# Attention's value product as two split float32r products on paired value halves, with row sums added up on GpSimd

## The reference, cut to what matters

```python
s_s = jnp.einsum('nqhd,nqkd->nqhk', q, ksel).astype(jnp.float32) * scale
p_s = masked_softmax(s_s, smask)
o_s = jnp.einsum('nqhk,nqkd->nqhd', p_s.astype(vsel.dtype), vsel)
...
o_w = jnp.einsum('nqhk,nkd->nqhd', p_w.astype(vw.dtype), vw)
return gates[..., 0:1] * o_c + gates[..., 1:2] * o_s + gates[..., 2:3] * o_w
```

## Time and profile before

| what | value |
|---|---|
| median of 3 runs | 2151.63 us (2148.56 to 2152.69) |
| profiled execution | 2151.09 us |
| its span | 2149.5 us |
| PE busy in the span | 1888.5 us (88%) |
| DVE, ACT, POOL busy | 1066.5, 616.8, 153.6 us |
| attention stage in the span | 1283 to 1745 us |

### The profile page before, as it was taken

How to read it: one execution, slowest core, us unless ns; L and a number is a source line. 1 busy time by engine, 2 the same in 40 slices (tenths; PEclk the granted TensorE clock), 3 DMA queues, 4 the chain that set the end, 5 groups by cost and what they waited for, 6 DMA issues and landing times. The chain is left out here.

```text
span 2149.5 us, 24334 instructions
## 1 busy us (share of the span) xinstructions
PE 1888.5 (88%) x8663; PEld 1347.1 (63%) x8663; DVE 1066.5 (50%) x2180; ACT 616.8 (29%) x1112; POOL 153.6 (7%) x264
## 2 busy tenths in 40 slices
PE   6799999999999999619996947899999978876999
PEld 1588878877877787406555633444445447875886
DVE  1376648746864775504464675455555422213332
ACT  3324343435334331303302522233333310002110
POOL 2101110000000000012210000000000021000000
PEclk9799999999999999857997667899999975557999
DMA  7537555545454544255223000000000032005331
GB/s 239 184 113 237 196 182 186 200 149 194 163 178 137 186 167 157 75 107 175 58 70 99 25 19 18 11 11 10 11 11 0 1 98 83 23 2 199 128 132 62
DMA packets 138776, 230.61 MB, mean 107 GB/s; under 512 B 14439, under 2 KB 90889, under 8 KB 138184
## 3 DMA queue, kind: packets, MB, share of 16 engines
q1 hardware_dynamic: 109525, 158.36, 23.1%
q0 software_dynamic: 17552, 57.22, 7.3%
q10 hardware_dynamic: 11579, 13.48, 2.0%
HBM read 175.27 MB, written 56.15 MB: 108 GB/s over the span
## 5 line engine op out<-in xcount | busy, mean ns | idle before, releaser
L578 PE MATMUL ps<-h_hi,w_hi 128*128 128x512 f32 x832 | 340.7, 410 | 0.0
L580 PE MATMUL ps<-h_lo,w_hi 128*128 128x512 f32 x832 | 325.1, 391 | 0.0
L579 PE MATMUL ps<-h_hi,w_lo 128*128 128x512 f32 x832 | 324.6, 390 | 0.0
L2114 PE MATMUL ps<-pT,values 128*65 128x512 f32 x412 | 216.8, 609 | 0.0
L2176 ACT ACTIVATE pT<-ps 128x512 f32<-128x512 f32 x206 | 123.0, 597 | 294.2 <-PE ps L2101 194.4
L2256 DVE TENSOR_REDUCE part_max<-ps 128x1 f32<-128x512 f32 (+3 forms) x272 | 143.0, 557 | 124.0 <-PE ps L2129 49.6
L920 DVE SCALAR_TENSOR_TENSOR c_acc<-c_u,par,c_acc 128x512 f32<-128x512 f32 x240 | 180.0, 750 | 6.8
L578 PEld LDWEIGHTS ps<-h_hi,w_hi 128*128 128x128 f32 x832 | 157.2, 189 | 35.9 <-issue 6.3
L579 PEld LDWEIGHTS ps<-h_hi,w_lo 128*128 128x128 f32 x832 | 157.1, 189 | 35.4 <-issue 5.8
L580 PEld LDWEIGHTS ps<-h_lo,w_hi 128*128 128x128 f32 x832 | 156.5, 188 | 34.0
L1344 PE MATMUL ps<-rawT,w 128*128 128x254 f32 (+1 forms) x320 | 137.5, 590 | 0.0
(11 more groups left out here) (594 smaller groups left out, 3170.6 us busy)
## 6 DMA issues: line engine op xcount, KB each, us to landing
w_hi<-split_weights SPq DMA_DIRECT2D x78, 512.0 KB, 3.7
w_lo<-split_weights SPq DMA_DIRECT2D x78, 512.0 KB, 4.6
w_raw<-in_w_in SPq DMA_DIRECT2D x26, 512.0 KB, 4.6
split_weights<-w_hi POOLq DMA_DIRECT2D x26, 512.0 KB, 5.5
split_weights<-w_lo POOLq DMA_DIRECT2D x26, 512.0 KB, 6.3
x_in<-in_x_prompt SPq DMA_DIRECT2D x4, 2048.0 KB, 11.2
tm<-in_x_prompt SPq DMA_DIRECT2D x16, 512.0 KB, 4.6
out_y_prompt<-y_out SPq DMA_DIRECT2D x16, 512.0 KB, 2.9
```

The source lines that it names most:

```text
L578: m.matmul(out, w_hi[:, b, kk, :], hh[:, kk, :], start=(kk == 0), stop=False)
L579: m.matmul(out, w_lo[:, b, kk, :], hh[:, kk, :], start=False, stop=False)
L580: return m.matmul(out, w_hi[:, b, kk, :], hl[:, kk, :], start=False, stop=(kk == KT - 1))
L2114: m.matmul(k.ps[0:VW, 5 + b, :], k.va[:, t, b, :], pT[:, i % NPT].rearrange("p h q -> p (h q)"), start=first, stop=end).then_inc(z["pv_don ...
```

## The change

The value product is done in float32r twice. `k.va` becomes float32r and holds for each chunk and branch two halves of 64 columns, the high part of the values and the rest, so that one product has 128 stationary columns: rows 0 to 63 of the bank gather the high values, rows 64 to 127 the rests. ScalarE computes each exponential twice, once into the float32r tile `p_hi` and once into the float32 tile `pT`; VectorE subtracts to get `p_lo`; TensorE multiplies the pair with `p_hi` and then with `p_lo`. The column of ones is gone; GpSimd adds `pT` of all tiles of a branch into `p_sum`. In the part step a float32 product with `twice` (two identity matrices stacked) transposes and adds the two halves, and another with a column of ones makes the row sums. `LAG` goes from 2 to 3 and `NPT` from 3 to 4.

```diff
--- before.py
+++ after.py
@@ -1927,9 +1927,10 @@
         def _(dve):
             v = nc.vector
             link = chain(dve, z["link"])
-            v.memset(k.va[:, :, :, HD:HD + 1], 1.0)
             for b in range(2):
-                last = v.tensor_copy(k.va[:, :, b, 0:HD], k.tm[:, 0:NC, 192 + 128 * b:256 + 128 * b])
+                src = k.tm[:, 0:NC, 192 + 128 * b:256 + 128 * b]
+                link(v.tensor_copy(k.va[:, :, b, 0, :], src))
+                last = v.tensor_tensor(k.va[:, :, b, 1, :], src, k.va[:, :, b, 0, :].bitcast(F32), ALU.subtract)
             last.then_inc(z["va_done"], 1)
             link(v.memset(pg[:, :, :], 0.0))
 
@@ -2004,7 +2005,7 @@
 
 
 
-    LAG, NST, NPT = 2, 3, 3
+    LAG, NST, NPT = 3, 3, 4
     VW = HD + 1
 
     def tiles_of(qb):
@@ -2053,8 +2054,11 @@
         FR, BF = mybir.dt.float32r, mybir.dt.bfloat16
         qhi, qboth = sb("q_hi", [P, 2, H * P], FR), sb("q_both", [P, 2, H * P], FR)
         q_raw = sb("q_raw", [P, 2, H * P])
-        pT = sb("pT", [P, NPT, H, P])
-        oT = sb("oT", [VW, 2, H * P])
+        pT = sb("pT", [P, NPT, H * P])
+        p_hi, p_lo = sb("p_hi", [P, NPT, H * P], FR), sb("p_lo", [P, NPT, H * P], FR)
+        p_sum = sb("p_sum", [P, 2, H * P])
+        oT = sb("oT", [P, 2, H * P])
+        twice = sb("twice", [P, HD])
         o_tm, o_part = sb("o_tm", [P, 2, W]), sb("o_part", [P, 2, W])
         part_max = sb("part_max", [P, 2, H, 4])
         shift = sb("row_shift", [P, H, 2])
@@ -2063,7 +2067,7 @@
         causal_b, low_b = (sb(n, [P, P], BF) for n in ("causal_b", "low_b"))
         lowT_b = sb("lowT_b", [P, H * P], BF)
         names = "ready q_done st_done exp_done pv_done misc_wr misc_rd mu_done mu_read bias_in shifted evac_sel evac_win summed link".split()
-        z = {n: sem("a_" + n) for n in names}
+        z = {n: sem("a_" + n) for n in names + ["hi_done", "lo_done", "sum_done"]}
         q_in = [sem("a_q0"), sem("a_q1")]
         block = ctx.enter_context(nc.Block())
         MISC = 7
@@ -2085,7 +2089,7 @@
         def _(pe):
             m = nc.tensor
             count = {"mu": 0}
-            pe.wait_ge(z["ready"], 4)
+            pe.wait_ge(z["ready"], 5)
 
             def scores(i):
                 qb, kind, t, first, _ = tiles[i]
@@ -2108,11 +2112,13 @@
                     return
                 qb, kind, t, first, end = tiles[i]
                 b = 0 if kind == "sel" else 1
-                pe.wait_ge(z["exp_done"], i + 1)
+                pe.wait_ge(z["hi_done"], i + 1)
                 if first and qb:
                     pe.wait_ge(z["evac_" + kind], qb)
-                m.matmul(k.ps[0:VW, 5 + b, :], k.va[:, t, b, :], pT[:, i % NPT].rearrange("p h q -> p (h q)"),
-                         start=first, stop=end).then_inc(z["pv_done"], 1)
+                pair = k.va[:, t, b].rearrange("p a d -> p (a d)")
+                m.matmul(k.ps[:, 5 + b, :], pair, p_hi[:, i % NPT], start=first, stop=False)
+                pe.wait_ge(z["lo_done"], i + 1)
+                m.matmul(k.ps[:, 5 + b, :], pair, p_lo[:, i % NPT], start=False, stop=end).then_inc(z["pv_done"], 1)
 
             def max_pass(qb, kind, h, a, b, col):
                 n = count["mu"]
@@ -2144,10 +2150,13 @@
                     for h in range(H):
                         last = m.transpose(bank[0:2, h * P:(h + 1) * P], shift[:, h, :], k.ident[:, :])
                 elif step in ("part_sel", "part_win"):
+                    b = 0 if step == "part_sel" else 1
                     pe.wait_ge(z["evac_" + step[5:]], qb + 1)
+                    pe.wait_ge(z["sum_done"], n_tiles[qb, step[5:]])
                     for h in range(H):
-                        last = m.transpose(bank[:, h * VW:(h + 1) * VW], oT[:, 0 if step == "part_sel" else 1, h * P:(h + 1) * P],
-                                           k.ident[0:VW, 0:VW])
+                        at, c = h * VW, slice(h * P, (h + 1) * P)
+                        m.matmul(bank[:, at:at + HD], oT[:, b, c], twice[:, :], start=True, stop=True)
+                        last = m.matmul(bank[:, at + HD:at + VW], p_sum[:, b, c], k.ones[:, 0:1], start=True, stop=True)
                 else:
                     pe.wait_ge(z["summed"], qb + 1)
                     for j in range(2):
@@ -2165,22 +2174,38 @@
                 elif what[0] == "max":
                     max_pass(n, *what[1:])
 
+        @block.gpsimd
+        def _(pool):
+            for i, (qb, kind, t, first, _) in enumerate(tiles):
+                b = 0 if kind == "sel" else 1
+                total = p_sum[:, b]
+                pool.wait_ge(z["exp_done"], i + 1)
+                if i:
+                    pool.wait_ge(z["sum_done"], i)
+                if first:
+                    if qb:
+                        pool.wait_ge(z["misc_rd"], misc_at["part_" + kind, qb - 1])
+                    nc.gpsimd.tensor_copy(total, pT[:, i % NPT]).then_inc(z["sum_done"], 1)
+                else:
+                    nc.gpsimd.tensor_tensor(total, total, pT[:, i % NPT], ALU.add).then_inc(z["sum_done"], 1)
+
         @block.scalar
         def _(act):
-            act.wait_ge(z["ready"], 4)
+            act.wait_ge(z["ready"], 5)
             for what, n in order:
                 if what == "tile":
                     act.wait_ge(z["st_done"], n + 1)
                     if n >= NPT:
                         act.wait_ge(z["pv_done"], n - NPT + 1)
-                    nc.scalar.activation(pT[:, n % NPT].rearrange("p h q -> p (h q)"), k.ps[:, n % NST, :], ACT.Exp,
-                                         scale=SCALE).then_inc(z["exp_done"], 1)
+                        act.wait_ge(z["sum_done"], n - NPT + 1)
+                    nc.scalar.activation(p_hi[:, n % NPT], k.ps[:, n % NST, :], ACT.Exp, scale=SCALE).then_inc(z["hi_done"], 1)
+                    nc.scalar.activation(pT[:, n % NPT], k.ps[:, n % NST, :], ACT.Exp, scale=SCALE).then_inc(z["exp_done"], 1)
                 elif what in ("evac_sel", "evac_win"):
                     b = 0 if what == "evac_sel" else 1
                     act.wait_ge(z["pv_done"], n_tiles[n, what[5:]])
                     if n:
                         act.wait_ge(z["misc_rd"], misc_at["part_" + what[5:], n - 1])
-                    nc.scalar.copy(oT[:, b, :], k.ps[0:VW, 5 + b, :]).then_inc(z[what], 1)
+                    nc.scalar.copy(oT[:, b, :], k.ps[:, 5 + b, :]).then_inc(z[what], 1)
                 elif what == "q":
                     if n >= 2:
                         act.wait_ge(z["st_done"], last_tile[n - 2] + 1)
@@ -2197,7 +2222,9 @@
             v.tensor_copy(low_b[:, :], k.win_low[:, :]).then_inc(z["ready"], 1)
             v.tensor_copy(lowT_b[:, :], k.low_T[:, :]).then_inc(z["ready"], 1)
             v.memset(part_max[:, :, :, :], 0.0).then_inc(z["ready"], 1)
-            dve.wait_ge(z["ready"], 4)
+            v.tensor_copy(twice[0:HD, :], k.ident[0:HD, 0:HD])
+            v.tensor_copy(twice[HD:P, :], k.ident[HD:P, HD:P]).then_inc(z["ready"], 1)
+            dve.wait_ge(z["ready"], 5)
 
             def misc(step, qb):
                 bank = k.ps[:, MISC, :]
@@ -2242,8 +2269,16 @@
                 v.tensor_tensor(qboth[low, qb % 2, :], q_raw[low, qb % 2, :], qhi[low, qb % 2, :].bitcast(F32),
                                 ALU.subtract).then_inc(z["q_done"], 1)
 
+            def rest_of(i):
+                dve.wait_ge(z["exp_done"], i + 1)
+                v.tensor_tensor(p_lo[:, i % NPT], pT[:, i % NPT], p_hi[:, i % NPT].bitcast(F32), ALU.subtract).then_inc(z["lo_done"], 1)
+
             for what, n in order:
-                if what == "q":
+                if what == "tile" and n:
+                    rest_of(n - 1)
+                elif what == "drain" and n == len(tiles):
+                    rest_of(n - 1)
+                elif what == "q":
                     queries(n)
                 elif what in MISC_STEPS:
                     misc(what, n)
@@ -2735,7 +2770,7 @@
                       for b in ("sel", "win")]
             run(stage_gather)
 
-            k.va = held.enter_context(nc.sbuf_tensor("values", [P, NC, 2, HD + 1], F32))
+            k.va = held.enter_context(nc.sbuf_tensor("values", [P, NC, 2, 2, HD], mybir.dt.float32r))
             k.biasT = held.enter_context(nc.sbuf_tensor("bias_T", [P, T], F32))
             run(stage_choice)
             run(stage_attention)
```

## The result

The changed kernel takes **2282.8 us** (median of 4 runs, 2277.2 to 2284.9) against 2151.0 before: ratio 1.061, interval 1.0595 to 1.0622. That is slower, as forecast, but +132 us where +55 was forecast, and outside the range. Its profiled execution has a span of 2275.6 us.

What follows compares the result with a forecast made beforehand. TensorE bounds attention's middle and end now; afterwards turns of subtraction and sum would. Middle 30, last block 14.5, start 8, end 2, filling `k.va` 0.6 make +55 on 2151.1: 2206 us, range of all cases 2132 to 2250.

Steps and rivals of the forecast that it cites:

- TensorE, 28 us saved: Attention: split value products save 76 us, dearer part steps cost 48, so TensorE alone saves 28.
- The price of the sum: GpSimd's 128x512 addition per tile was taken at 1.22 us, between bounds of 0.61 and 1.22.
- The turns: GpSimd's sum and VectorE's subtraction, both reading SBUF, take turns each tile: 1.91 us plus 0.11 hand-over.
- The turns ask 2.20, so 330 us, +30: Middle 300 us, 150 tiles: turns, hand-over and block-level VectorE operations need 2.20 us a tile instead of 2.00.
- The lower clock: In the third rival: less regular work could also lower TensorE's granted clock, 0.78 where it was 81% busy; no price.
- filling `k.va`: Before attention: two subtractions of 1024 elements minus the memset add 2.4 us, of which +0.6 remains after VectorE's idle time.
- The third lag step and the fourth buffer cover that: Per tile: the second exponential delays `exp_done` by half a microsecond, hidden by the greater depth at no cost.
- 28 x 0.69 = 19 at most: First 117 us, 28 tiles: bound on subtractions delaying maxima TensorE awaits; +8 taken for the start, between -5 and +35.
- They pass each other: Rival: sum and subtraction collide only now and then, below 1.85 us a tile together; 2139 us, chance 0.22.
- The sum is cheap: Rival: GpSimd's sum takes 0.61 us, so turns ask 1.59 a tile; 2152 us, no difference, chance 0.10.
- The subtraction waits out a sum at most tiles: Rival: VectorE waits half or a whole sum per tile, middle +57 or +148; 2233 to 2324 us, chance 0.13.
- The signs to look for: Products 0.24 apart, part steps near 1.9 us, sums near 1.2 alone, last-block steps 2.0, TensorE idle before the value product.

Runs made afterwards that it cites:

- e_nosum_part: Changed kernel with GpSimd adding only 8 of 512 columns per tile and the old part step of four transposes; 2137.6 us.
- e_nosum: Changed kernel with GpSimd adding only 8 of the 512 columns of each tile; 2199.4 us.
- e_lag2: Changed kernel with two lag steps instead of three, four buffers kept; 2289.5 us.
- c_ones: Changed kernel with a column of ones replacing value column 63's lower half, no GpSimd sum, four part-step products of 65 columns; 2153.8 us.
- c_lag2: The c_ones version with two lag steps instead of three; 2137.9 us.
- b_stall: Kernel before, with VectorE filling a spare tile and adding it to itself three times before negating each block's row maxima; 2227.2 us.

## Why the prediction was wrong, step by step

- **TensorE, 28 us saved: right.** The work of the stage fell by 29 us (406 to 377). Both terms hold: 77 us for the split products (e_nosum_part against before), 46 for the part steps (48 forecast). Products of the last block that wait for nothing start 0.23 to 0.24 apart.
- **The price of the sum: right.** 1.26 us alone for 1.22; the Trainium skill's figure (GPSIMD Engine Reference, 3.1 Elementwise), 1.12, was a little low here.
- **The turns: the mechanism right, their size too large, their effect misread.** In the last block the pair takes 1.69 us a tile, not 2.02:

```profile
1840.76 0.50 PE L2121 MATMUL ps<-p_lo,values 128*128 128x512 f32 x1 [0.49 <-DVE p_lo L2274]
...
1842.45 0.50 PE L2121 MATMUL ps<-p_lo,values 128*128 128x512 f32 x1 [0.49 <-DVE p_lo L2274]
```

  and the records of the subtraction and of the sum, min/median/max in ns, between 1839 and 1852 us:

```profile
L2274 DVE TENSOR_TENSOR p_lo<-pT,p_hi x9: 1253/1769/1772, 1837.8 to 1850.8; 128x512 fp32r<-128x512 f32 x9
...
L2190 POOL TENSOR_TENSOR p_sum<-p_sum,pT x8: 1545/1550/1553, 1838.6 to 1850.5; 128x512 f32<-128x512 f32 x8
```

  Alone the two are 0.69 + 1.26 = 1.95, so 0.26 us overlap. Each waits for the other here, not GpSimd alone. The subtraction that starts at 1840.63 finds a sum that ends at 1841.85 and itself ends 0.55 after it; the sum that starts at 1840.30 ends 1.14 after the subtraction before it. So each gets its first 0.12 to 0.14 us done beside the other. The Trainium skill (SBUF — State Buffer, Who interferes with whom) has whoever starts first hold the path for its whole instruction. The trace agrees in both directions, except for those 0.26 us a pair. From the first to the last of the block's 21 exponentials it is 34.3 us for 28.0, +6.3, where +14.5 was summed.
- **"The turns ask 2.20, so 330 us, +30": the step that failed.** It made the pair's time per tile the pace of the middle and treated TensorE as always able to follow at full clock. The turns did not fill the middle (GpSimd 142 of 300 us, TensorE waiting 6.2 us for the low probabilities in the whole stage). Their price came where a block's few steps follow one another without cover, above all at the queries: a cast that finds a sum running waits it out, the query wait went from 10.6 to 28.4 us, and behind it lie 101 of the middle's 149 us at half clock, nearly all of which go with the sums (e_nosum). The shift wait went from 13.8 to 33.2 us, but most of that is not the turns: it is 27.1 without the sums, and 27.3 in the kernel before at depth 3. Over the stage that is +50 idle and +104 clock; the sum had 83 for the first (its +55 and the 28 that TensorE saves) and nothing for the second. The lower clock stood in one sentence of a rival, without a price. Term by term, from the starts of the exponentials: up to the 28th +24 (+8 summed), from there to the last block +92 (+30), last block +6 (+14.5), end +4 (+2); for filling `k.va` nothing is left to find (+0.6).
- **"The third lag step and the fourth buffer cover that": costed at nothing, and wrong.** Depth 3 put the part step on the shift step's tile, worth 26 us in the kernel before and 16 in the version with the column of ones (c_ones to c_lag2). In the changed kernel itself, going back to depth 2 gave nothing (e_lag2), so its share in the +132 is not shown. The order's slots were in the code and could have been counted beforehand.
- **"28 x 0.69 = 19 at most" for the start**: by 1400 us the changed kernel had done 23 exponential pairs instead of 30 exponentials, and the clock there was 0.60 instead of 0.78. The 28th started at 1418.2 instead of 1394.3, +24: inside the bounds given (-5 to +35), 16 over the +8 taken.
- **The rivals.** "They pass each other" and "The sum is cheap" fall. The first had its sign, under 1.85 us for the pair (1.69), and the middle still took 2.58 us a tile and not under 2: the pair's pace did not decide. "The subtraction waits out a sum at most tiles" covered the time, 2233 to 2324, by luck: that happened in the last block, but only at 35 of the 185 tiles before it, and its price was worked out from the pace of the tiles, not from the clock.
- **The signs to look for** held, all but two: last-block steps (1.69, not 2.0), and TensorE idle mainly before the shift and the queries and not before the value product.

How the +132 splits, in the order in which the runs undo it: without the sums -83; then without the dearer part step -62; what is left, 2137.6, is 13 under the kernel before. In the other order it is -33 and -112: a step freed while another still holds VectorE back only makes TensorE wait.

## What to carry to other kernels

Price a new wait of TensorE by what it does to the granted clock, not by its length alone: in the kernel before, 2 to 3 us more of standstill at each block cost 1.8 times themselves (b_stall), and in the changed kernel 50 us more of idle time came with 104 us lost to the clock. Before moving a depth or a lag, write out which steps then fall on the same tile, and which engine does them one after the other. And an operation that two engines share a path for is best judged where nothing covers it (between blocks), not by the mean per tile; taking one operand from PSUM freed the subtraction here, though the queries' operations still met the sums; letting a column of ones in the product do the sum removed the sharing.

## What the runs showed that was not expected

- A gap with no other change (b_stall) cost 76 us for 42 us of idle time.
- A VectorE operation with a single SBUF input, the cast of 64x512, had a mean of 1.13 to 1.14 us beside GpSimd's 1.26 us sums and takes 0.42 without; each such cast ended 0.28 us after the sum that it had found running. The sharing is not confined to operations with two SBUF inputs. With two, even one of 128x4 waits: 0.57 us at 1609.48, with a sum running up to 1610.03, and 0.17 in the kernel before.
- TensorE idle 31 of 300 us at a clock of 1.00 (c_lag2), 35 at 0.92 (b_stall) and 37 at 0.75 (changed kernel): the sum of the idle time does not tell the clock. Nor does the longest gap: 1.56 us and then 1.08 in each block of c_lag2, 3.5 alone in b_stall, 2.1 to 2.8 and then mostly 0.9 to 2.2 in the changed kernel. What does was not isolated.
